# Modulation row of a fused three-layer transformer kernel: twelve partition sums in one column group or in four

## What is computed

```python
c_act = jax.nn.silu(c)                       # c is 1 x 1024
ada = c_act @ w_ada[l] + b_ada[l]            # 1 x 6144 (w_ada: 1024 x 6144)
shift_a, scale_a, gate_a, shift_m, scale_m, gate_m = jnp.split(ada, N_ADA, axis=-1)
h = modulate(rmsnorm(x, g_mix[l]), shift_a, scale_a)
...
x = x + gate_a[:, None, :] * y
```

## Time and profile before

| | |
|---|---|
| device time, three runs | 1855.85, 1857.75, 1861.78 us |
| profiled execution, first to last instruction | 1859.6 us, within the range of the three runs |
| TensorE matmul busy | 1801.0 us (97%) |
| VectorE busy | 1419.1 us (76%) |
| ScalarE busy | 1110.9 us (60%) |
| GpSimd busy | 129.0 us (7%) |
| DMA | 525.78 MB, mean 283 GB/s |
| the twelve sums on TensorE (L2947) | 24 matmul records, 10.8 us busy, between 357.4 and 376.1 us |

### The profile page before, as it was taken

The page is one execution under the profiler, slowest core; times in us unless marked ns, Lnnn a source line. Parts: engine busy times, 40 slices in busy tenths (PEclk is TensorE's granted clock), DMA queues, the critical chain, the costliest instruction groups (busy, mean ns, idle before and its releaser), DMA issues.

```text
span 1859.6 us, 22581 instructions
## 1 busy us (share of the span) xinstructions
PE 1801.0 (97%) x8518; PEld 1476.5 (79%) x8526; DVE 1419.1 (76%) x1255; ACT 1110.9 (60%) x1018; POOL 129.0 (7%) x148
## 2 busy tenths in 40 slices
PE   7979999999989999999999999999999989899998
PEld 6867888778768888888888888888887768778886
DVE  5557778757768888889888888888889964466556
ACT  6654344453447777777777777777777734533333
POOL 3010111022110000000000000000001020100000
PEclk9979999999989999999999999999999999989999
DMA  9636899653249999999999999999999964335550
GB/s 320 212 109 221 289 332 324 223 169 114 98 164 374 377 386 382 376 385 381 378 384 376 389 380 378 383 366 383 375 375 397 360 211 136 102 113 184 189 192 24
DMA packets 238109, 525.78 MB, mean 283 GB/s; under 512 B 17850, under 2 KB 41546, under 8 KB 237872
## 3 DMA queue, kind: packets, MB, share of 16 engines
q1 hardware_dynamic: 224432, 477.29, 71.6%
q0 software_dynamic: 13568, 47.07, 7.5%
HBM read 513.77 MB, written 10.53 MB: 282 GB/s over the span
## 4 chain that ended last, share of the span: by engine, by line
PE 91%; DVE 4%; ACT 2%; DMA 1%; issue 1%; POOL 0%; SPq 0%; DVEq 0%; ACTq 0%; POOLq 0%
PE bank L2627 27%; PE bank L2628 27%; PE bank L2635 27%; PE bank L2775 2%; PE bank L3065 1%; ACT w_hi L986 1%; DVE w_lo L1587 1%; DMA raw<-in_moe_w_gate_up 1%; PE bank L2681 1%; PE bank L2737 1%; DMA raw<-in_a_w_mem_kv 1%; PE bank L2688 1%; PE bank L2947 0%; PE bank L3332 0%; POOL mix L934 0%
## 5 line engine op out<-in xcount | busy, mean ns | idle before, releaser
L1587 DVE TENSOR_TENSOR w_lo<-raw,w_hi 128x2048 fp32r<-128x2048 f32 x454 | 1041.0, 2295 | 227.2 <-ACT w_hi L986 219.8
L986 ACT ACTIVATE w_hi<-raw 128x2048 fp32r<-128x2048 f32 x454 | 867.5, 1912 | 492.6 <-PE bank L2628 365.7
L2627 PE MATMUL bank<-w_hi,slot_hi 128*128 128x512 f32 x896 | 357.0, 398 | 2.6 <-ACT w_hi L986 2.6
L2628 PE MATMUL bank<-w_hi,slot_lo 128*128 128x512 f32 x896 | 351.1, 392 | 0.0
L2627 PE MATMUL bank<-w_hi,hT_hi 128*128 128x512 f32 (+2 forms) x728 | 287.7, 396 | 5.1 <-ACT w_hi L986 4.2
L2628 PE MATMUL bank<-w_hi,hT_lo 128*128 128x512 f32 (+2 forms) x728 | 282.5, 389 | 0.0
L2635 PE MATMUL bank<-w_lo,slot_hi 128*128 128x512 f32 x896 | 240.9, 391 | 0.9 <-DVE w_lo L1587 0.9
L2635 PEld LDWEIGHTS bank<-w_lo,slot_hi 128*128 128x128 f32 x896 | 168.5, 188 | 38.1 <-DVE w_lo L1587 2.7
L2627 PEld LDWEIGHTS bank<-w_hi,slot_hi 128*128 128x128 f32 x896 | 169.1, 189 | 37.0 <-issue 3.0
L2628 PEld LDWEIGHTS bank<-w_hi,slot_lo 128*128 128x128 f32 x896 | 169.4, 189 | 33.5
L2627 PE MATMUL bank<-w_hi,e_hid_hi 128*128 128x512 f32 x444 | 173.7, 391 | 4.4 <-DVE e_hid_lo L2195 4.4
(11 more groups left out here) (382 smaller groups left out, 1476.2 us busy)
## 6 DMA issues: line engine op xcount, KB each, us to landing
raw<-in_moe_w_gate_up SPq DMA_DIRECT2D x448, 512.0 KB, 5.6
raw<-in_moe_w_down SPq DMA_DIRECT2D x224, 512.0 KB, 5.6
raw<-in_w_ff SPq DMA_DIRECT2D x64, 512.0 KB, 4.4
work<-in_w_ada POOLq DMA_DIRECT2D x48, 512.0 KB, 5.5
raw<-in_dense_w_gate_up SPq DMA_DIRECT2D x44, 512.0 KB, 5.0
raw<-in_b_w_in SPq DMA_DIRECT2D x24, 512.0 KB, 5.0
raw<-in_w_in SPq DMA_DIRECT2D x24, 512.0 KB, 4.8
raw<-in_dense_w_down SPq DMA_DIRECT2D x22, 512.0 KB, 4.8
```

Source lines behind the costliest of these rows:

```text
L986: act.activation(w_hi[:, g % SPLIT, 0:n], raw[:, g % RING, 0:n], ACT.Copy).then_inc(R.hi, 1)
L1587: dve.tensor_tensor(w_lo[:, g % SPLIT, 0:n], raw[:, g % RING, 0:n], f32(w_hi[:, g % SPLIT, 0:n]), ALU.subtract).then_inc(R.lo, 1)
L2627: pe.matmul(out_, hi, w_hi[:, s, c:c + w], start=(start and n == 0), stop=False, skip_group_check=True)
L2628: mm = pe.matmul(out_, lo, w_hi[:, s, c:c + w], start=False, stop=False, skip_group_check=True)
```

## The change

`sum_ada` deals the twelve products out to four groups of 32 columns of the array. Product j goes to group j % 4 and lands in PSUM partitions 32 (j % 4) to 32 (j % 4) + 31, in row j // 4 of them; the stationary window is 32 columns wide, in place of 12. Each group accumulates three products. Neighbours in the order are always of different groups. The calls move as well: four products (0 to 3) stand ahead of `turn_first`, none behind it, and the last eight stay where they were.

The row now lies on partitions 0 to 2, 32 to 34, 64 to 66 and 96 to 98. GpSimd clears the whole 128x512 place first and waits for that, loads the bias by four transfers of 3x512 in place of one of 12x512, and stores by four as well; the waits on their semaphores ask for four landings. VectorE adds 128x512 in place of 12x512.

```diff
         def ada_place():
-            return work[0:2 * N_ADA, 9216:9728]
+            return work[:, 9216:9728]
+        def ada_rows_of(quad):
+            return work[32 * quad:32 * quad + ADA_TURNS, 9216:9728]
+        def by_quad(rows):
+            return rows.rearrange("(r q) n -> q r n", q=QUADS)
...
-            pool.dma_start(ada_place(), A["b_ada_2"].rearrange("l (a n) -> (l a) n", n=512)).then_inc(ada_bias_in, 16)
+            pool.memset(ada_place(), 0.0).then_inc(ada_cleared, 1)
+            pool.wait_ge(ada_cleared, 1)
+            for quad in range(QUADS):
+                pool.dma_start(ada_rows_of(quad), by_quad(A["b_ada_2"].rearrange("l (a n) -> (l a) n", n=512))[quad])\
+                    .then_inc(ada_bias_in, 16)
...
-            pool.dma_start(ada_dram, ada_place()).then_inc(ada_stored, 16)
+            for quad in range(QUADS):
+                pool.dma_start(by_quad(ada_dram)[quad], ada_rows_of(quad)).then_inc(ada_stored, 16)
...
-                    pool.wait_ge(ada_stored, 16)
+                    pool.wait_ge(ada_stored, 16 * QUADS)
...
-                        act.wait_ge(ada_stored, 16)
+                        act.wait_ge(ada_stored, 16 * QUADS)
...
-                    dve.tensor_tensor(ada_place(), ada_place(), bank[2][0:2 * N_ADA, :], ALU.add).then_inc(S("ada", "row"), 1)
+                    dve.tensor_tensor(ada_place(), ada_place(), bank[2][:, :], ALU.add).then_inc(S("ada", "row"), 1)
...
                     for j in range(first, last):
-                        mm = pe.matmul(bank[2][0:2 * N_ADA, :], one_row[:, 2 * N_ADA - 1 - j:4 * N_ADA - 1 - j],
-                                       work[:, j * 512:(j + 1) * 512], start=(j == 0), stop=(j == 2 * N_ADA - 1), skip_group_check=True)
+                        quad, turn_ = j % QUADS, j // QUADS
+                        mm = pe.matmul(bank[2][32 * quad:32 * quad + 32, :], one_row[:, ADA_TURNS - 1 - turn_:ADA_TURNS + 31 - turn_],
+                                       work[:, j * 512:(j + 1) * 512], start=(turn_ == 0), stop=(turn_ == ADA_TURNS - 1),
+                                       skip_group_check=True)
...
                     pe.wait_ge(ada_ready, ADA_ROWS)
-                    sum_ada(0, 2)
+                    sum_ada(0, QUADS)
                 turn_first()
-                if have("ada"):
-                    sum_ada(2, 4)
...
                         if (j, h) == (0, 0) and have("ada"):
-                            sum_ada(4, 2 * N_ADA)
+                            sum_ada(QUADS, 2 * N_ADA)
```

More of the change, by code:

```diff
@@ L59 @@
 N_ADA = 6
+QUADS = 4
+ADA_TURNS = 2 * N_ADA // QUADS
 ADA_BUFFERS = 3
@@ L187, in program @@
         c_col = sb("c_col", [P, KC])
-        one_row = sb("one_row", [P, 4 * N_ADA - 1])
+        one_row = sb("one_row", [P, 32 + ADA_TURNS - 1])
         sumsq = sb("sumsq", [P, TILES])
@@ L309, in program @@
         ada_bias_in = semaphore("ada_bias_in")
+        ada_cleared = semaphore("ada_cleared")
         ada_stored = semaphore("ada_stored")
@@ L834, in _ @@
             pool.memset(ones[:, :], 1.0)
-            pool.memset(one_row[:, 0:2 * N_ADA - 1], 0.0)
-            pool.memset(one_row[:, 2 * N_ADA:], 0.0)
-            pool.memset(one_row[:, 2 * N_ADA - 1:2 * N_ADA], 1.0)
+            pool.memset(one_row[:, 0:ADA_TURNS - 1], 0.0)
+            pool.memset(one_row[:, ADA_TURNS:], 0.0)
+            pool.memset(one_row[:, ADA_TURNS - 1:ADA_TURNS], 1.0)
             pool.memset(zero[:, :], 0.0).then_inc(S("zero"), 1)
@@ L1997, in _ @@
                 if have("ada"):
-                    dve.wait_ge(ada_bias_in, 16)
+                    dve.wait_ge(ada_bias_in, 16 * QUADS)
                     dve.wait_ge(*at("ada", "summed"))
-                    dve.tensor_tensor(ada_place(), ada_place(), bank[2][0:2 * N_ADA, :], ALU.add).then_inc(S("ada", "row"), 1)
+                    dve.tensor_tensor(ada_place(), ada_place(), bank[2][:, :], ALU.add).then_inc(S("ada", "row"), 1)
                 def inside(j):
```

## The result

The changed kernel takes 1883.95 us (median of four runs, 1883.65 to 1886.32) against 1858.57 us for the kernel before, measured beside it (1855.85 to 1861.78). The ratio is 1.0129, with a 95% interval of 1.0113 to 1.0144. The forecast was 1853.9 us, within a range up to 1860.

What follows compares the result with a forecast made beforehand. TensorE, holding 91% of the 1859.6 us span, was taken to bound the kernel. From the median 1857.75, -5.1 - 0.44 + 1.7 = -3.85 us gave 1853.9 us, range 1850.5 to 1860.

Steps and rivals of the forecast that it cites:

- Part 1: Eight products between the steps: four column groups run side by side, 1.72 us against 6.88; 5.1 us saved.
- Rival 2: In the sums, matmuls start in program order, so n products take n + 1 starts; 1856.9 us, chance 0.25.
- Rival 3: In the sums, nothing runs side by side; +3.4 us with the clock at half, 1861.2 us, chance 0.15.
- Weight loads: In the sums: four loads per 430 ns would take 0.37 us, just covered, so no limit.
- Part 2: Four products ahead of the turns, none behind: turns begin 0.96 us earlier, first step gains 0.44 us.
- Part 3: Ahead of the first step TensorE idles 2.7 us, then its clock halves for 3.4 us; 1.7 us lost.
- six gaps out of six: Evidence for the clock's fall: behind all six idle gaps of 2.2 us or more, the clock is about half.
- rival 1: Ahead of the first step, the 2.7 us idling isn't punished; -5.5 us, 1852.2 us, chance 0.13.
- Part 4: GpSimd's clearing, extra bias transfers, VectorE's wider add and the four-issue store are covered and cost nothing.
- the sum: Whole kernel: -5.1 - 0.44 + 1.7 = -3.85 us from the median 1857.75, with all streams shifting together behind the sums.

Runs made afterwards that it cites:

- e9: e6 with product j in group j // 3, so neighbours mostly share a group; 1860.36 us, ratio 1.0000 to the kernel before.
- e6: The changed kernel with 48 unused columns behind one_row, tiles behind it 256 bytes further on than before; 1854.80 us, ratio 0.9965 to the kernel before.
- e8: The kernel before with unused columns setting hT, dense hid, slot and e_hid to distances 96, 160, 192, 224 from w_hi modulo 256 bytes; 1880.92 us, single run.
- e1: The kernel before with an unused tile of 16 columns behind one_row, moving everything behind it by 64 bytes; 1885.55 us against 1861.77.
- e4: The kernel before with 16 unused columns ahead of w_hi and 16 behind w_lo, shifting moving operands 64 bytes against stationary ones; 1900.06 us, ratio 1.0198.
- e10: The kernel before, still one group, with four products ahead of the turns and none behind; 1865.21 us, ratio 1.0027.
- e5: The kernel before with 16 unused columns ahead of w_hi, moving and stationary operands all shifted by 64 bytes; 1862.34 us against 1861.36.
- e2: The changed kernel with 16 unused columns behind one_row, tiles behind it 128 bytes further on than before; 1881.91 us, ratio 1.0102 to the kernel before.

## Why the prediction was wrong

- **Part 1, the eight products: right.** 5.1 us were forecast and 6.96 - 1.85 = 5.1 measured. The matmuls of four groups start 6 to 8 ns apart, then some 430 ns later the next four; the two row groups of the earlier trace rows carried over to four column groups. Rival 2, starts in program order, is refuted: the five and nine starts it asked for were two and four. Rival 3, nothing side by side, is refuted by the same starts. The rule of the Trainium skill ("TensorE: Matmul & The Clock Gate", Part 3) that matmuls start strictly in order does not hold between column groups here: in e9 a product starts 0.85 us ahead of one that stands before it, and overtaking ends after three or four matmuls.
- **Weight loads: no limit, as forecast, but not for its reason.** The prediction laid four loads end to end, 0.37 us of each 0.43, "just covered". With 32 columns one load takes 109 ns in place of 93, and end to end four would take 436 ns, more than 430. But they overlap: four pass in 0.13 us, and the loader is idle for 0.30 before them:

```profile
L2964 PEld LDWEIGHTS bank<-work,one_row x24: 106/109/110, 362.8 to 376.5; 128*32 128x32 f32 x24
376.02 0.13 PEld L2964 LDWEIGHTS bank<-work,one_row 128*32 128x32 f32 x4 [0.30 <-issue]
```

- **Part 2, the turns: right.** The first step comes 4.55 us behind the first sum in place of 5.10; 0.55 gained for 0.44. VectorE's squares of `x` (L1646) were indeed next, and `hT_lo` starts right behind them, without the idle time that it had in the earlier trace rows:

```profile
364.54 1.23 DVE L1646 CUSTOM_DVE_ANT_0 mix<-x 128x1024 f32<-128x1024 f32 x1
365.69 1.66 DVE L1668 SCALAR_TENSOR_TENSOR hT_lo<-bank,gain_col,hT_hi 128x256 fp32r<-128x256 f32 x4
```

- **Part 3, the gap and the clock: right in size, too sure.** 2.46 us for 2.7, and 1.57 us for 1.7 where the clock fell. But six gaps out of six in one trace were one execution. Behind the gap of this change it held in e6; behind the gap of 2.58 us ahead of the first `slot_hi`, one of the six, it held in e8 and e9. And the trace before had a seventh gap, at its start, which the count left out: 3.40 us of idling, and a granted clock of 1.00 behind it. Its row of the timeline, and the stretch behind it with columns as in the earlier trace rows:

```profile
14.57 0.47 PE L2627 MATMUL bank<-w_hi,hT_hi 128*128 128x512 f32 x1 [3.40 <-ACT w_hi L986]
14.60:18.00 3.40, 3.40 (x15) 2.83 (x16) 3.40 (x5) 2.01 (x5) 0.00 (x0) 1.00 1.09 255
```

- **The rival that came true** in e6, with the layout restored, is rival 1, "the clock holds": 6.6 us gained by the times and 5.62 by the profile, where that rival had 5.5 and a chance of 0.13. How often the clock holds there is open: five runs, of which one was profiled.
- **Part 4, what costs nothing: right for all that it lists.** The clearing took 0.52 us, and the store is done 6.8 us before ScalarE's early turns want it:

```profile
140.87 0.52 POOL L652 MEMSET work<- 128x512 f32 x1 [31.46 <-DVE mix L1735]
378.61 1.99 POOL L664 DMA_DIRECT2D ada_dram<-work  x4 [28.40 <-DVE work L2016]
382.35 3.56 POOL L891 DMA_DIRECT2D late_col<-ada_dram  x4 [1.75 <-DMA ada_dram<-work]
389.16 1.28 ACT L1092 ACT_TABLE_LOAD   x1 [0.33 <-PE bank L2722]
```

- **The step that failed is the sum.** It adds the four parts to the old time and says that "behind the sums all streams shift together". That takes for granted that some 6,800 other matmuls cost what they cost before. The diff has a line that none of the parts priced: the width of `one_row`. It moved three stages' stationary operands by 64 bytes, and e1 shows that this alone is 24 us, four times all that the sums had to give. No rival had it, so the range could not hold it. That the change shifts tiles could have been read from the declarations; that a shift has a price could not be read from the trace of before, in which all these operands are at the same distance from the moving ones, modulo 256 bytes, and all large matmuls some 227 ns apart, whatever the stage.
- The size is not fully accounted for. Some 4,640 matmuls times 6.6 ns is 30.6 us, and e1 took 24; for e4 the same reckoning gave 46, and 38 came. Both are a fifth short. In e1's profile the shortfall lies in the experts: 20.9 us more over 4,032 matmuls, 5.2 ns each, while the 384 large matmuls of ff_2's `hid2` took 161.1 in place of 158.5 us from the first to the last, 6.9 ns each. Why it is less in the experts is open.
- The changed kernel lost more than e1 and the gain of the sums together allow: 25.4 us, where 24 less 4 to 6.6 would be 17 to 20. The intervals just meet. The mean granted clock is lower in its runs, 0.9798 against 0.9825 in e1's, and at the 1.2 us for each 0.001 that e10's neighbours show this is an estimated 3 us; the rest is within the spread.

## What to carry to other kernels

When a kernel is bound by matmuls, the addresses of its tiles are part of it: after any edit to a declaration compare where the stationary and moving tiles lie, and pad so that the distance stays what it was. If a change is slower than its trace says at the place it touches, take the distance of matmul starts per operand far away from it; an unused tile in the old kernel settles in one run whether it is the layout. Products of 32 columns do run four abreast in fp32, if neighbours in program order are of different groups.

## What the runs showed of the hardware

- 128x128 by 128x512 matmuls on fp32r operands start 226.7 ns apart (mean with `e_hid`; 227 to 229 with other tiles) if the stationary tile is a multiple of 256 bytes away from the moving one, and 229.5 to 234.2 ns apart at the seven other distances in steps of 32 bytes. Moving all operands together by 64 bytes changed nothing (e5). That stationary and moving reads meet in memory would explain it, but only the distances were tried.
- fp32 matmuls of 512 columns, two to a product: one of each of four groups of 32 columns took 430 ns together, the same as one alone; a matmul of another group overtakes three or four older ones, not five (e9, counted as said there).
- Loads of 32-column weights for four groups overlap: 109 ns each, four in 0.13 us.
- Behind an idle gap of about 2.5 us TensorE's granted clock fell to half for some 3.4 us in the profiles of the changed kernel and e2, and not in that of e6; behind one of 2.19 us it fell in e9 and not in e10, and behind one of 3.40 us at the start of the kernel before it didn't fall.
